# A two-layer diffusion trunk on one core: weights laid out piece by piece as contiguous blocks in HBM

## What is computed

```
for layer 0, 1:
    m = silu(c) @ ada_w[l] + ada_b[l]          # six 1024-wide vectors: shift, scale, gate, twice
    h = rms(x) * (1 + scale) + shift
    layer 0: z = h @ w_in; attention (8 heads, w_qb, w_kvb) beside a 3-tap gated convolution; @ w_o
    layer 1: h @ conv_pw1 (1024 -> 2048), gate, 31-tap depthwise convolution, layernorm, @ conv_pw2
    x = x + gate * out
    h = rms(x) * (1 + scale2) + shift2
    layer 0: (silu(h @ ffn_gu[:, :2816]) * (h @ ffn_gu[:, 2816:])) @ ffn_down
    layer 1: top 2 of 8 experts per token, each the same with width 3584 (moe_gu, moe_down)
    x = x + gate2 * out
```

## Time and profile before

| | |
|---|---|
| time, three runs | 1747.69, 1750.07, 1752.91 us; median 1750.07 |
| span of the profiled execution | 1752.1 us |
| PE, PEld busy | 89%, 71% |
| DVE, ACT, POOL busy | 70%, 56%, 1% |
| moved by DMA | 471.62 MB in 340,212 packets, mean 269 GB/s |
| from 700 us to the end | the eight experts, 130 us each |

### The profile page before, as it was taken

The page is one execution under the profiler, slowest core; times in us unless marked ns, Lnnn a source line. Parts: engine busy times, 40 slices in busy tenths (PEclk is TensorE's granted clock), DMA queues, the critical chain, the costliest instruction groups (busy, mean ns, idle before and its releaser), DMA issues.

```text
span 1752.1 us, 20909 instructions
## 1 busy us (share of the span) xinstructions
PE 1564.9 (89%) x7157; PEld 1235.7 (71%) x7157; DVE 1231.9 (70%) x1171; ACT 973.2 (56%) x978; POOL 18.6 (1%) x25
## 2 busy tenths in 40 slices
PE   3758878999598877999999999999999999999996
PEld 1536556888476555788788788788788788788784
DVE  1444555544558726788888888888888888888886
ACT  1232424443435533677677677676676776776673
POOL 0000000000000000000000000000000000000000
PEclk9778889999798977999999999999999999999998
DMA  7554685565344515899999999999999999999992
GB/s 273 184 189 173 221 277 175 190 192 192 120 145 144 199 41 192 284 362 334 315 366 335 316 366 336 318 366 333 318 366 336 308 366 334 324 366 318 327 364 100
DMA packets 340212, 471.62 MB, mean 269 GB/s; under 512 B 13023, under 2 KB 274861, under 8 KB 340158
## 3 DMA queue, kind: packets, MB, share of 16 engines
q1 hardware_dynamic: 336176, 464.43, 77.8%
q0 software_dynamic: 1216, 4.28, 0.7%
q10 hardware_dynamic: 2766, 2.22, 0.4%
HBM read 469.75 MB, written 1.13 MB: 269 GB/s over the span
## 4 chain that ended last, share of the span: by engine, by line
PE 82%; DVE 10%; ACT 4%; DMA 2%; issue 1%; ACTq 0%; POOL 0%; DVEq 0%; POOLq 0%
PE bank L1395 23%; PE bank L1397 23%; PE bank L1396 23%; DVE low L1307 2%; PE bank L1407 2%; PE bank L1770 2%; ACT high L741 2%; PE bank L1884 2%; PE bank L1912 1%; DVE low L814 1%; DVE hid L1159 1%; PE bank L1424 1%; DMA x<-x_sample 1%; PE bank L1443 1%; ACT high L468 1%
## 5 line engine op out<-in xcount | busy, mean ns | idle before, releaser
L1307 DVE TENSOR_TENSOR low<-raw,high 128x2048 fp32r<-128x2048 f32 x333 | 760.6, 2292 | 150.5 <-ACT high L741 137.6
L741 ACT ACTIVATE high<-raw 128x2048 fp32r<-128x2048 f32 x333 | 634.6, 1915 | 111.9 <-PE bank L1397 111.3
L1395 PE MATMUL bank<-high,slotH 128*128 128x512 f32 x896 | 359.1, 401 | 26.2 <-DVE low L1307 25.4
L1397 PE MATMUL bank<-high,slotL 128*128 128x512 f32 x896 | 356.9, 398 | 0.0
L1396 PE MATMUL bank<-low,slotH 128*128 128x512 f32 x896 | 356.0, 397 | 0.0
L1395 PE MATMUL bank<-high,upH 128*128 128x512 f32 (+1 forms) x550 | 227.6, 414 | 4.4 <-DVE upL L944 2.8
L1395 PEld LDWEIGHTS bank<-high,slotH 128*128 128x128 f32 x896 | 169.1, 189 | 73.7 <-DVE low L1307 33.8
L1397 PE MATMUL bank<-high,upL 128*128 128x512 f32 (+1 forms) x550 | 217.3, 395 | 0.0
L1396 PE MATMUL bank<-low,upH 128*128 128x512 f32 (+1 forms) x550 | 215.3, 391 | 0.0
L814 DVE TENSOR_TENSOR low<-raw,high 128x2048 fp32r<-128x2048 f32 (+3 forms) x59 | 132.3, 2250 | 106.8 <-ACT high L468 106.6
L1397 PEld LDWEIGHTS bank<-high,slotL 128*128 128x128 f32 x896 | 169.3, 189 | 40.8
(11 more groups left out here) (228 smaller groups left out, 1221.2 us busy)
## 6 DMA issues: line engine op xcount, KB each, us to landing
raw<-moe_gu SPq DMA_DIRECT2D x448, 512.0 KB, 5.4
raw<-moe_down SPq DMA_DIRECT2D x112, 1024.0 KB, 6.6
raw<-ada_w SPq DMA_DIRECT2D x48, 1024.0 KB, 7.0
raw<-ffn_gu SPq DMA_DIRECT2D x44, 512.0 KB, 4.9
raw<-ffn_down SPq DMA_DIRECT2D x11, 1024.0 KB, 4.9
raw<-conv_pw SPq DMA_DIRECT2D x16, 512.0 KB, 4.4
raw<-w_in SPq DMA_DIRECT2D x6, 1024.0 KB, 8.0
raw<-w_o SPq DMA_DIRECT2D x4, 1024.0 KB, 6.8
```

The source lines that it names most:

```text
L741: a.activation(high[:, m % SPLITS, :], raw[:, n % RAWS, :], ACT.Copy).then_inc(S("high_ready"), 1)
L1307: v.tensor_tensor(low[:, m % SPLITS, :], raw[:, n % RAWS, :], high[:, m % SPLITS, :].bitcast(F32), ALU.subtract).then_inc(S("low_ready"), 1)
L1395: pe.matmul(out, xh, wh, start=start, stop=False)
L1397: return pe.matmul(out, xl, wh, start=False, stop=stop)
```

## The change

The weights now reach the chip in two new arrays, filled on the host by copying alone: `dense`, one block of 1 MB for each of the 107 pieces of `ORDER`, and `moe`, one block for each of the 8 x 42 expert pieces. In a block the 8 KB of one partition are contiguous, in the very order that `raw` wants. Each load is then one transfer of 128 rows. `win` chunk 0, `qb` and `kvb` are narrower and load only the first part of each row. The waits count 16 for every piece, so that all six slots have the same count, 112 for each expert. No computing instruction, no ring and no order of the pieces changes.

```diff
-                kind = piece[0]
-                if kind in ("ffn", "pw1") and piece[1] != "d":
-                    w, ff = (t["ffn_gu"][0], D_FF) if kind == "ffn" else (t["conv_pw1"][0], D)
-                    dst = w_slot(raw, slot, (KH, 2, UNIT))
-                    g, u = gu_parts(w, ff, piece[2], "ab".index(piece[1]))
-                    sp.dma_start(dst[:, :, 0, :], g).then_inc(arrived, 16)
-                    sp.dma_start(dst[:, :, 1, :], u).then_inc(arrived, 16)
-                    return 32
...
-                sp.dma_start(dst, src).then_inc(arrived, 16)
-                return 16
+                w = width(piece)
+                sp.dma_start(raw[:, slot, 0:w], t["dense"][n, :, 0:w]).then_inc(arrived, 16)
...
-                if kind == "d":
-                    src = t["moe_down"][0].rearrange("e (u c p) n -> e u p c n", p=P, c=UC)
-                    sp.dma_start(w_slot(raw, slot, (UC, D)), src[bass.ds(e, 1), u]).then_inc(arrived, 16)
-                else:
...
-                    sp.dma_start(dst[:, :, 0, :], v[:, :, :, c0:c0 + UNIT]).then_inc(arrived, 16)
-                    sp.dma_start(dst[:, :, 1, :], v[:, :, :, D_FFE + c0:D_FFE + c0 + UNIT]).then_inc(arrived, 16)
+                sp.dma_start(raw[:, slot, :], t["moe"][bass.ds(e, 1), i]).then_inc(arrived, 16)
...
         def arrived_value(n):
-            return 16 * sum(loads_of(ORDER[m]) for m in range(n % RAWS, n + 1, RAWS))
+            return 16 * (n // RAWS + 1)
...
         def expert_value(first, i):
-            slot = (first + i) % RAWS
-            within = sum(16 if STREAM_E[m][0] == "d" else 32 for m in range(i + 1) if (first + m) % RAWS == slot)
-            per = sum(16 if STREAM_E[m][0] == "d" else 32 for m in range(PER_E) if (first + m) % RAWS == slot)
...
+            return 16 * ((first + i) // RAWS + 1), 16 * (PER_E // RAWS)
```

More of the change, by code:

```diff
@@ L261, in width @@
             return PIECE
[L263 to L269, removed]
         def product(eng, *piece):
@@ L288, in load @@
                         sp.wait_ge(S("low_ready"), NUM[last] + 1)
-                kind = piece[0]
-                if kind in ("ffn", "pw1") and piece[1] != "d":
-                    w, ff = (t["ffn_gu"][0], D_FF) if kind == "ffn" else (t["conv_pw1"][0], D)
-                    dst = w_slot(raw, slot, (KH, 2, UNIT))
-                    g, u = gu_parts(w, ff, piece[2], "ab".index(piece[1]))
-                    sp.dma_start(dst[:, :, 0, :], g).then_inc(arrived, 16)
-                    sp.dma_start(dst[:, :, 1, :], u).then_inc(arrived, 16)
-                    return 32
[L297 to L313, removed]
-                else:
-                    w = t["w_o"][0] if kind == "wo" else t["conv_pw2"][0]
-                    dst = w_slot(raw, slot, (KH, 512))
-                    src = col_part(w, piece[2], piece[1] * 512, 512)
-                sp.dma_start(dst, src).then_inc(arrived, 16)
-                return 16
+                w = width(piece)
+                sp.dma_start(raw[:, slot, 0:w], t["dense"][n, :, 0:w]).then_inc(arrived, 16)
             for n, piece in enumerate(ORDER):
@@ L324, in expert_load @@
             def expert_load(e, first, i, free):
-                kind, u = STREAM_E[i]
                 slot = (first + i) % RAWS
@@ L371, in _ @@
             sp.wait_ge(S("y_out"), 32)
-        def loads_of(piece):
-            return 2 if piece[0] in ("ffn", "pw1") and piece[1] != "d" else 1
         def arrived_value(n):
-            return 16 * sum(loads_of(ORDER[m]) for m in range(n % RAWS, n + 1, RAWS))
-        def slot_total(slot):
-            return 16 * sum(loads_of(ORDER[m]) for m in range(slot, N_DENSE, RAWS))
+            return 16 * (n // RAWS + 1)
         def expert_value(first, i):
-            slot = (first + i) % RAWS
-            within = sum(16 if STREAM_E[m][0] == "d" else 32 for m in range(i + 1) if (first + m) % RAWS == slot)
-            per = sum(16 if STREAM_E[m][0] == "d" else 32 for m in range(PER_E) if (first + m) % RAWS == slot)
-            passes = (first - N_DENSE) // (EXPERTS * PER_E)
-            return slot_total(slot) + passes * EXPERTS * per + within, per
+            return 16 * ((first + i) // RAWS + 1), 16 * (PER_E // RAWS)
         @block.gpsimd
@@ L1972, in _ @@
                 experts(N_DENSE + EXPERTS * PER_E, N_SPLIT + EXPERTS * PER_E, 1)
[L1975 to L1978, removed]
+NAMES = ["x_prompt", "x_sample", "cache_ckv", "cache_kpe", "c", "c_ctx", "ada_b", "norm_mix", "norm_ffn",
+         "q_a_norm", "kv_a_norm", "q_norm", "k_norm", "w_sc", "conv_pw1_b", "conv_dw", "conv_dw_b", "conv_ln_g", "conv_ln_b", "conv_pw2_b",
+         "router"]
 def constants():
@@ L2004, in constants, with rows_of, gate_up_rows, down_rows @@
     return c
+def rows_of(w, kh, c0, cw):
+    return w[kh * KH * P:(kh + 1) * KH * P, c0:c0 + cw].reshape(KH, P, cw).transpose(1, 0, 2)
+def gate_up_rows(w, ff, u, kh):
+    import numpy as np
+    return np.stack([rows_of(w, kh, u * UNIT, UNIT), rows_of(w, kh, ff + u * UNIT, UNIT)], axis=2)
+def down_rows(w, u):
+    return w[u * UNIT:(u + 1) * UNIT].reshape(UC, P, D).transpose(1, 0, 2)
+def dense_piece(inputs, piece):
+    kind = piece[0]
+    if kind == "ada":
+        (l, c), kh = piece[1], piece[2]
+        return rows_of(inputs["ada_w"][l], kh, c * 512, 512)
+    if kind == "win":
+        c0, cw = W_CHUNK[piece[1]]
+        return rows_of(inputs["w_in"][0], piece[2], c0, cw)
+    if kind == "qb":
+        return inputs["w_qb"][0].reshape(2, P, HEADS * QK).transpose(1, 0, 2)
+    if kind == "kvb":
+        return inputs["w_kvb"][0]
+    if kind == "ffn":
+        if piece[1] == "d":
+            return down_rows(inputs["ffn_down"][0], piece[2])
+        return gate_up_rows(inputs["ffn_gu"][0], D_FF, piece[2], "ab".index(piece[1]))
+    if kind == "pw1":
+        return gate_up_rows(inputs["conv_pw1"][0], D, piece[2], "ab".index(piece[1]))
+    w = inputs["w_o"][0] if kind == "wo" else inputs["conv_pw2"][0]
+    return rows_of(w, piece[2], piece[1] * 512, 512)
 def kernel(**inputs):
@@ L2014 @@
     arrays["table"] = constants()
+    dense = np.zeros((N_DENSE, P, PIECE), np.float32)
+    for n, piece in enumerate(ORDER):
+        rows = np.asarray(dense_piece(inputs, piece)).reshape(P, -1)
+        dense[n, :, 0:rows.shape[1]] = rows
+    moe = np.empty((EXPERTS, PER_E, P, PIECE), np.float32)
+    for e in range(EXPERTS):
+        w_gu, w_down = np.asarray(inputs["moe_gu"][0, e]), np.asarray(inputs["moe_down"][0, e])
+        for i, (kind, u) in enumerate(STREAM_E):
+            rows = down_rows(w_down, u) if kind == "d" else gate_up_rows(w_gu, D_FFE, u, "ab".index(kind))
+            moe[e, i] = rows.reshape(P, PIECE)
+    arrays["dense"], arrays["moe"] = dense, moe
     t = {name: nc.dram_tensor(name, arr.shape, F32, kind="ExternalInput").ap() for name, arr in arrays.items()}
```

## The result

The changed kernel took 1759.01 us (median of 6 runs, 1754.15 to 1759.74), the kernel before 1749.56 in the runs beside it. The ratio is 1.0047, 95% interval [1.0031, 1.0062]. So it is slower by 5 to 9 us. The forecast was +4, with turns by packet as the cause and a slower rival at +8.6. The mechanism held and its sizes were too small.

A forecast was written before the change was run, and what follows sets the result against it. The prediction took PE to bound the experts, with only three transfers on the chain. Its terms, 2.0 - 0.5 + 3.0 - 0.5 = +4.0 us, put on the median of 1750.07, gave 1754 us (+0.23%), range 1746 to 1761.

The forecast's parts named there:

- turns by packet: Shared DMA engines: queues alternate one whole packet at a time, so others get one turn per 8 KB of weights, not 2 KB.
- a slower rival at +8.6: Start and gate: x at the very end of traffic (+4.6), gate at its bound (+4.5), less 0.5; 1759 us, chance 0.21.
- The experts are bound by PE: Experts, 1040 of 1752 us: ACT waits for PE, never for loads; faster loads only lower the DMA share.
- Row stays one packet: Weight loads: an 8 KB row stays one packet, giving about 64,000 packets on q1, against about 121,000 if cut.
- the rival with two packets of 4 KB: Weight loads: 8 KB rows cut in two; start and gate +1 each, 1751 us; within the forecast's class, together 0.64.
- The start, +2.0: Kernel start: `x_sample` lands later, at 24.7 instead of 22.72 us, costing +2.0 us (bounds -1.0 and +4.6).
- the stuck issues: Kernel start: SP's 5.4 us stuck in an issue might also cost ACT's issues; used for the start's lower bound, -1.0.
- The `w_in` piece, -0.5: Awaited `w_in` load at 124.39 us: larger rows land it sooner, -0.5 us (bounds -1.0 and 0).
- The gate, +3.0: Gate's `ada_b` load at 212.39 us: gets a smaller share beside weight loads, +3.0 us (bounds -2.1 and +4.5).
- Register operations, -0.5: ACT's sequencer in the experts: one operation may go at each of 16 places, -0.5 us (bounds -1.0 and 0).
- within 0.3%: Whole kernel: time not told from no change, within 0.3% or 5.3 us; class "same", chance 0.66.
- slower, 0.24: Whole kernel: chance 0.24 that the change comes out slower; the rival of slower by turns had 0.21, slow packets 0.03.

The follow-up runs named there:

- experiment 2: The changed kernel with each full 1 MB block written as two runs of 4 KB a partition instead of 8 KB rows: 1753.43 us, 1.0022 against the kernel before.
- experiment 6: The changed kernel (8 KB rows) with ACT loading x first and the gate's `ada_b` loaded once for both token tiles: 1747.46 us, 0.9985 against the kernel before.
- the second, 1754.71: The changed kernel measured again, unaltered, beside the kernel before: 1754.71 us (12 runs), ratio 1.0030.

## Why the prediction was right, and where it was too small

*The experts are bound by PE, and faster loads bring nothing there.* Right: PE busy unchanged, the distance of the traces the same at both ends of 880 us, and over the experts' copies no wait of ACT for a load.

*Row stays one packet.* Right, 64,080 packets against about 64,000. So the rival with two packets of 4 KB is out. The Trainium skill ("DMA: Bandwidth & Descriptors", section "SWDGE vs HWDGE vs iDMA") gives 4096 B as the preferred largest packet. These loads do not keep to it: the queue's 64,080 packets and the 214 to 212 at the gate fit rows of 8 KB that stay whole.

*The start, +2.0.* Measured +2.5; x came at 25.2 us, just past the 24 to 25 that was to be seen. Right in size. (In its working, 0.65 x 64 / 0.783 gives 53 and not 83; the 83 ns come from the bracket behind it, and the sum uses those.) The path was only half seen: I had x arriving late behind the weights, but not ACT's issues stuck for 4.35 and 2.39 us. By experiment 2 these did not delay x, but in experiment 6 such an issue was what bound. I even put the stuck issues on the other side, as something that could get better. SP's did (its longest of the first six had been 5.4 us); ACT's became the worse ones.

*The `w_in` piece, -0.5.* Measured -0.5, the shift between the two traces goes from -2.47 ahead of it to -2.99 behind it; the four loads issued there landed in 4.9 us at the least, where the awaited piece had taken 5.35.

*The gate, +3.0.* The landing took 3.1 us more, PE's wait 3.1. The shift over the place is 4.0 us, from -2.75 to +1.21, so 0.9 came on top. It goes with a longer stretch of half clock right behind the wait: 6.8 us from 225.0 us, where before it was 3.4 from 227.6. The prediction had no term for it. DVE's wait was 6.7 us, near the 6.5 that was to be seen.

*Register operations, -0.5.* Nothing to be seen. With the measured sizes the sum is +6, not +4: 2.5 - 0.5 + 4.0. The mis-sized terms are the gate, 1.0 too small, the start, 0.5 too small, and the register operations, put at a gain of 0.5 that did not come.

*The rest.* +6 lies between the two medians of +5.6 and +9.5 us, and beside the 5.2 and 6.1 us by which the ends of all runs moved. What is above 6 in the first measurement is not explained by any load. The six spans of that session stand in two groups 5 us apart, and the two profiled traces differ by 4.1 us in one stretch with half clock after 40 us. That this is the difference of the groups is supported by the mean clocks of the runs, which go with their times, but not shown: no run of the slower group of the changed kernel was traced. The forecast number was 5 us low against the first measurement, 1754 for 1759.01, and met the second, 1754.71; both lie inside its range. By the differences from the kernel before it was low by 5.5 and by 1.6 us. The likeliest class was "within 0.3%"; the first ratio, 1.0047, lies outside it and the second, 1.0030, on its edge. So the weight on slower, 0.24, was too small. The steps together had an upper bound of 8.6, and I should have asked how much of that weight lies over 5.3 when the central value is already 4.

## What to carry to other kernels

Before you make a transfer more efficient, ask whether anyone waits for it; here nearly all of the 443 weight loads got larger packets, and only one of them stood on the chain. Then look at who shares the engines: with queues that take turns by packet, making one queue's packets four times larger takes turns from every other, and the small loads at a kernel's start and in its seams are those on the path. If large packets are wanted, issue the critical small loads first and hold the bulk until they have landed; here both together took the 8 KB version from 1754.7 to 1736.8 us, though small packets with the same cures and no hold came within 1.3 us of that.

## What was not expected of the hardware

A queue that gets few turns can hold up the engine that issues on it, not only its data: one issue on ACT took 10.03 us beside 8 KB packets and 1.73 beside 2 KB ones, where the first ones, on an empty queue, took 0.3 to 0.8. And the half-clock stretch after 40 us is of different length in executions of closely like kernels, and with it went 4 us here. That is more than most of the effects that were to be measured, and runs of one kernel lie up to 10 us apart; so 6 to 12 runs of each kernel left intervals 0.3 to 0.5% wide.
